# Writing out the two rounds of each kind of layer, one behind the other, on every engine

## The reference

```python
for l in range(DEPTH):            # first kind
    h = rms_norm(x, attn_norm_g[l]); proj = h @ w_in[l]            # 1024 x 3584
    ret = retention_bidir(...)      # 8 heads, with decays
    da = diff_attention(...)        # 4 heads, two softmaxes each
    x = x + concatenate([ret, da]) @ w_out[l]
    h = rms_norm(x, ffn_norm_g[l])
    x = x + (silu(h @ w_gate[l]) * (h @ w_up[l])) @ w_down[l]      # 2816 wide
for l in range(DEPTH):            # second kind
    # four branches (three kinds of attention and a convolution of 31 taps),
    # each gated and projected, then w_o
    x = x + sum(gates * proj) @ w_o[l]
    x = x + square(relu(rms_norm(x) @ w_up[l])) @ w_down[l]        # 4096 wide
return rms_norm(x, g_final)
```

## Time and profile before

| | before |
|---|---|
| time, median of 3 runs | 1469.72 us (1469.54 to 1470.15) |
| the profiled execution's own time | 1470.93 us |
| its span | 1469.1 us |
| TensorE (PE) busy | 1443.7 us, 98% of the span |
| weight loads (PEld) busy | 1202.3 us, 82% |
| VectorE busy | 942.9 us, 64% |
| ScalarE busy | 782.5 us, 53% |
| GpSimd busy | 95.9 us, 7% |
| granted TensorE clock | 0.998 of full speed |

### The profile page before, as it was taken

One profiled execution on the slowest core, in us unless ns is written; L12 is line 12 of the kernel. 1 busy time (PEld: TensorE's weight loads), 2 busy tenths in 40 slices (PEclk: granted clock), 3 DMA queues, 4 the chain that ended last, 5 costly groups with the idle time before them and its releaser, 6 DMA issues.

```text
span 1469.1 us, 21875 instructions
## 1 busy us (share of the span) xinstructions
PE 1443.7 (98%) x7107; PEld 1202.3 (82%) x7107; DVE 942.9 (64%) x1120; ACT 782.5 (53%) x1013; POOL 95.9 (7%) x112
## 2 busy tenths in 40 slices
PE   8999999999999999999999999999999999999997
PEld 6788888888788888887888888888878888888885
DVE  5765655446756555446788878755366888787644
ACT  6665544446855444446675555544366765565442
POOL 0211000002111000000210000000002200000000
PEclk9999999999999999999999999999999999999999
DMA  8533755555435655545454666555454556665641
GB/s 319 172 127 115 229 184 188 181 185 171 148 112 175 197 186 178 186 144 190 144 166 158 204 205 201 189 188 181 160 183 135 167 160 192 204 212 186 201 143 43
DMA packets 173641, 257.48 MB, mean 175 GB/s; under 512 B 8456, under 2 KB 92002, under 8 KB 173410
## 3 DMA queue, kind: packets, MB, share of 16 engines
q1 hardware_dynamic: 170432, 249.74, 52.2%
q10 hardware_dynamic: 2962, 5.95, 1.3%
q0 software_dynamic: 144, 0.52, 0.1%
HBM read 255.13 MB, written 1.05 MB: 174 GB/s over the span
## 4 chain that ended last, share of the span: by engine, by line
PE 72%; issue 23%; DVE 2%; ACT 1%; POOL 1%; DMA 0%; ACTq 0%; POOLq 0%; DVEq 0%
PE bank L501 19%; PE bank L503 18%; PE bank L502 18%; PE bank L977 4%; PE bank L535 4%; PE bank L976 2%; PE bank L666 1%; PE bank L518 1%; PE bank L520 1%; PE bank L519 1%; PE bank L623 1%; PE bank L649 1%; ACT w_hi L1039 1%; PE bank L640 0%; PE bank L816 0%
## 5 line engine op out<-in xcount | busy, mean ns | idle before, releaser
L1536 DVE TENSOR_TENSOR w_lo<-w_raw,w_hi 128x2048 fp32r<-128x2048 f32 (+2 forms) x250 | 545.6, 2187 | 223.0 <-ACT w_hi L1039 219.7
L1039 ACT CAST w_hi<-w_raw 128x2048 fp32r<-128x2048 f32 (+2 forms) x250 | 454.2, 1825 | 227.8 <-PE bank L503 203.9
L501 PE MATMUL bank<-w_hi,hT 128*128 128x512 f32 (+1 forms) x1056 | 418.6, 396 | 0.9 <-issue 0.7
L503 PE MATMUL bank<-w_hi,hT 128*128 128x512 f32 (+1 forms) x1056 | 411.2, 389 | 0.0
L502 PE MATMUL bank<-w_lo,hT 128*128 128x512 f32 (+1 forms) x1056 | 410.8, 389 | 0.0
L501 PEld LDWEIGHTS bank<-w_hi,hT 128*128 128x128 f32 x1056 | 198.8, 188 | 41.6 <-issue 3.0
L503 PEld LDWEIGHTS bank<-w_hi,hT 128*128 128x128 f32 x1056 | 198.6, 188 | 41.4
L502 PEld LDWEIGHTS bank<-w_lo,hT 128*128 128x128 f32 x1056 | 199.0, 188 | 37.9
L977 PE MATMUL bank<-hT,w_hi 128*128 128x512 f32 x512 | 178.1, 396 | 0.4 <-DVE sum L2091 0.4
L976 PE MATMUL bank<-hT,w_lo 128*128 128x256 f32 x448 | 125.1, 279 | 0.0
L2151 POOL TENSOR_TENSOR stat<-stat,cst 128x2 f32<-128x2 f32 (+3 forms) x23 | 45.8, 1992 | 1151.3 <-DVE stat L1585 1012.8
(11 more groups left out here) (269 smaller groups left out, 1643.3 us busy)
## 6 DMA issues: line engine op xcount, KB each, us to landing
w_raw<-in_w_gate SPq DMA_DIRECT2D x108, 512.0 KB, 4.0
w_raw<-in_w_up SPq DMA_DIRECT2D x108, 512.0 KB, 4.7
w_raw<-in_w_down SPq DMA_DIRECT2D x104, 512.0 KB, 4.4
w_raw<-in_w_in SPq DMA_DIRECT2D x88, 512.0 KB, 4.5
w_raw<-in_w_out SPq DMA_DIRECT2D x16, 512.0 KB, 4.2
w_raw<-in_w_branch SPq DMA_DIRECT2D x32, 256.0 KB, 3.0
w_raw<-in_w_o SPq DMA_DIRECT2D x16, 512.0 KB, 4.6
bgate<-in_b_gate ACTq DMA_DIRECT2D x16, 256.0 KB, 3.6
```

The source lines that it names most:

```text
L501: pe.matmul(o, hi[:, kt, rows_of(r)], w_hi[:, s, j, 0:cols], start=begin, stop=False)
L503: mm = pe.matmul(o, lo[:, kt, rows_of(r)], w_hi[:, s, j, 0:cols], start=False, stop=end)
L1039: act.copy(w_hi[:, s, 0:kts, :], w_raw[:, s, 0:kts, :]).then_inc(hi_ready, 1)
L1536: dve.tensor_tensor(w_lo[:, s, 0:kts, :], w_raw[:, s, 0:kts, :], w_hi[:, s, 0:kts, :].bitcast(F32), ALU.subtract).then_inc(lo_ready, 1)
```

## The change

`Place` gets a second generator, `layers`, which runs the body of a layer twice in Python and makes no loop of the hardware. All ten outer loops (two on each of SP, PE, ACT, DVE and POOL) use it in place of `rounds`; the arguments stay, and serve only for an assertion. The inner loops still use `rounds`. So `l` is a plain number, the counts on which the engines wait are constants outside the inner loops, slices such as `gcols[:, bass.ds(l * 16 + kt, 1)]` have a constant place, and there is no jump at a layer's end.

```diff
--- before.py
+++ after.py
@@ -174,6 +174,14 @@
         self.base = base
         self.k = {x: k.get(x, 0) + n * per.get(x, 0) for x in {*k, *per}}
+
+    def layers(self, per):
+
+        for l in range(DEPTH):
+            k = dict(self.k)
+            yield l
+            grown = {x: self.k[x] - k.get(x, 0) for x in self.k if self.k[x] != k.get(x, 0)}
+            assert grown == {x: y for x, y in per.items() if y}, (self.e, grown, per)
@@ -396,7 +404,7 @@
-            for l in q.rounds(DEPTH, dict(slab=len(KTS1))):
+            for l in q.layers(dict(slab=len(KTS1))):
@@ -610,7 +618,7 @@
-            for l in q.rounds(DEPTH, dict(slab=len(KTS1), blk=BLOCKS1, turn=TURNS1, scores=16, dve=9)):
+            for l in q.layers(dict(slab=len(KTS1), blk=BLOCKS1, turn=TURNS1, scores=16, dve=9)):
...
```

More of the change, by code:

```diff
@@ L423, in _ @@
                         slab(*rows(w["w_down"], k0, min(4, 22 - k0), b * NB, NB))
-            for l in q.rounds(DEPTH, dict(slab=len(KTS2))):
+            for l in q.layers(dict(slab=len(KTS2))):
                 w = {n: t[n + "_2"][bass.ds(l, 1)].rearrange("o k n -> (o k) n")
@@ L791, in _ @@
             q.next("probs", DEPTH * DH)
-            for l in q.rounds(DEPTH, dict(slab=len(KTS2), blk=BLOCKS2, turn=TURNS2, scores=12, pool=2, dve=6, hid=UPS,
+            for l in q.layers(dict(slab=len(KTS2), blk=BLOCKS2, turn=TURNS2, scores=12, pool=2, dve=6, hid=UPS,
                                           layer_in=64, probs=12, conv=1, out=3)):
@@ L1123, in _ @@
             loop4 = dict(slab=4, used=4, blk=2, **{f"in{s}": 16 for s in range(RING)})
-            for l in q.rounds(DEPTH, per1):
+            for l in q.layers(per1):
                 ahead = iter(KTS1[AHEAD:] + KTS1[:AHEAD])
@@ L1308, in _ @@
                         **{f"in{s}": 16 * len(KTS2) // RING for s in range(RING)})
-            for l in q.rounds(DEPTH, per2):
+            for l in q.layers(per2):
                 ahead = iter(KTS2[AHEAD:] + KTS2[:AHEAD])
@@ L1662, in _ @@
             loop4 = dict(slab=4, used=4, blk=2)
-            for l in q.rounds(DEPTH, dict(slab=len(KTS1), used=len(KTS1), blk=BLOCKS1, turn=TURNS1,
+            for l in q.layers(dict(slab=len(KTS1), used=len(KTS1), blk=BLOCKS1, turn=TURNS1,
                                           turn_hi=4 + 4 + 11 + 4, squares=9, rstd=7, act_done=11, scores=16,
@@ L1839, in _ @@
                 add_x(1)
-            for l in q.rounds(DEPTH, dict(slab=len(KTS2), used=len(KTS2), blk=BLOCKS2, turn=TURNS2,
+            for l in q.layers(dict(slab=len(KTS2), used=len(KTS2), blk=BLOCKS2, turn=TURNS2,
                                           turn_hi=2 + 4 + 4 + 4 + 4, squares=5, rstd=4, act_done=10, hid=UPS, scores=12,
@@ L2161, in _ @@
             pool.wait_ge(ident_in, 16)
-            for l in q.rounds(DEPTH, dict(mean=7, outputs=2, decay=RH, blk=BLOCKS1, step=STEPS_POOL1)):
+            for l in q.layers(dict(mean=7, outputs=2, decay=RH, blk=BLOCKS1, step=STEPS_POOL1)):
                 def diagonals(heads):
@@ L2192, in _ @@
                 q.next("blk", BLOCKS1)
-            for l in q.rounds(DEPTH, dict(mean=4, blk=BLOCKS2, step=STEPS_POOL2)):
+            for l in q.layers(dict(mean=4, blk=BLOCKS2, step=STEPS_POOL2)):
                 root_x()
```

## The result

| | before | after |
|---|---|---|
| median | 1469.76 us (1469.16 to 1470.2, 6 runs) | 1476.35 us (1473.9 to 1479.31, 6 runs) |
| ratio after / before | | 1.0043 (95%: 1.0032 to 1.0054) |
| the profiled execution's own time | 1470.93 us | 1479.31 us |
| its span | 1469.1 us | 1477.5 us |
| granted clock in it | 0.998 | 0.995 |

The changed kernel is 0.43% slower: 6.6 us more, where 1.5 us less had been forecast. The result lies outside the range.

What follows compares the result with a forecast made beforehand. PE was taken to bound the kernel; 1.06 us from its jumps plus 0.5 us from register instructions and waits made 1.56 us, so 1468.2 us from the median 1469.72, range 1466.0 to 1470.3, counted as no change.

Steps and rivals of the forecast that it cites:

- What bounds the kernel, and the gap at 1051 us: TensorE busy 1443.7 of 1469.1 us, clock granted in full; PE's weight loads lose 1.04 us to a jump at layer's end.
- PE's two jumps back: At the ends of PE's two first layers: removing the jumps gains 1.04 + 0.02 = 1.06 us, bounds 0 and 1.06.
- The jumps of the other engines: Layer ends on SP, ACT and DVE: removing these jumps is worth 0, being covered; uncovered, up to 4.6 us.
- Register instructions and constant waits: Hand-overs to PE: some 1250 instructions removed shorten six slow places by 0.08 us each, 0.5 us gain, bounds 0 and 3.2.
- Added code: PE's program grows from 5810 to 10984 instructions: costs 0, or 1.04 us if a new block came late once.
- Inner loops: Loops inside the layers keep the same bodies at other places of the program: taken as 0.
- slower: Rival, 8%: PE's short inner-loop jumps become long, each uncovering 1.04 us; all twelve give 1480.6 us.
- The waits are worth more: Rival, 10%: hand-overs shorten by more than 0.08 us as ACT and DVE lose register instructions; at the bound 1465.4 us.
- Nothing comes back: Rival, 20%: the gap at 1051 closes, but PE waits at the next hand-over instead; 1469.3 to 1469.8 us.
- The signs named at its end: Changed profile: no PE jump over 1 us, busy time within 1 us, span 1 to 2 us shorter, named waits within 0.1.

Runs made afterwards that it cites:

- experiment 3: Outer loops written out on PE alone, all other engines as in the kernel before: 1469.73 us, ratio 0.9993.
- Experiment 4: The changed kernel with ACT's outer loops kept as hardware loops, all other engines written out: 1469.82 us, ratio 0.9996.
- 1: The changed kernel with one ACT semaphore increment between the two waits of every gate: 1470.6 us, ratio 0.9999.
- 6: The changed kernel with the gate's two waits written in the other order, no instruction added: 1469.11 us, ratio 0.9992.
- 5: Outer loops written out on ACT alone, all other engines as in the kernel before: 1478.15 us, ratio 1.0061.
- 7: The changed kernel with an ACT semaphore increment between the two waits in only the first of a layer's eight gates: 1474.44 us, ratio 1.0030.
- 11: The changed kernel with an ACT semaphore increment between the two waits in gates 2 to 8, not the first: 1471.88 us, ratio 1.0014.
- experiment 2: The kernel before, loops kept, with an ACT semaphore increment behind both waits of the gate, so the table load follows both: 1475.79 us, ratio 1.0041.

## Why the prediction was wrong, point by point

- **What bounds the kernel, and the gap at 1051 us**: right. PE sets the time, and the gap was the jump. That the clock is "granted in full in every slice" reads too much into the page, whose digit 9 means 90% or more: the changed kernel's page has a 9 in every slice too, with two low stretches in it.
- **PE's two jumps back, 1.06 us of gain**: right at its place, 1.04 us shown in the changed kernel, and gone in experiment 3 too. Of the whole kernel's time the median of 3 shows a gain of 0.0007 of it, 1.0 us, with an interval that includes nothing.
- **The jumps of the other engines, 0**: nothing in these runs speaks against it. Experiment 4 takes them away on SP, DVE and POOL, together with PE's, and reads as 3 does.
- **"Register instructions and constant waits", +0.5 us, bounded by 0 and 3.2 us of gain**: this is the step that failed. It priced register instructions by the time that they take, and asked only how quickly a released wait gets through. It did not ask which instruction a wait moves to when the one that carried it is gone. At ACT's gates the late wait moved ahead of a table load of 1.28 us, twelve times. The loss of 6.6 us isn't in the bounds since no bound had a loss in it. The two bits of evidence could be had: ACT's rows of the program's order at the gate, and the overlap at 723.11 us in the trace of before; ACT's rows were read at the start of the first kind of layer alone, where the fold of five `ISA` and one `REGISTER_ALU` was taken as a gain. The prediction's small term itself came out as reckoned where the gates don't disturb it. At the gated sum the hop from DVE's signal to PE is 0.04 us where the earlier trace rows had 0.12, and PE's idle time there is 0.54 us in experiments 1, 4 and 6 where it was 0.61; at the hidden sum it is 0.44 where it was 0.51. What the term left out beside this: at the branch the same kernels stand 1.85 to 1.87 us where it was 1.71.
- **Added code, 0**: right. Experiment 3 has PE's 10984 instructions and loses nothing, and product follows product at the steady pace.
- **Inner loops, 0**: right, 76 to 240 ns.
- **The rivals**: "slower" had the right sign and the wrong mechanism (long jumps in inner loops; none is there). "The waits are worth more" expected the hand-overs to shrink as ACT loses register instructions; the opposite came. "Nothing comes back" is how the change would read with the gate's waits in order: experiments 1 and 6 come out within 0.1% of before.
- **The signs named at its end**: the jumps came out as said. PE's busy time and the span did not (3.1 and 8.4 us more). The waits on L1561 and `abias` were to keep within 0.1 us and did about (in all 2.9 us after 2.6, and 1.2 after 1.1); the list missed the waits for `qB` and `soft`, where the loss was.
- **Not foreseen at all**: that stalls can be followed by a stretch at the low clock. In the profiled execution it makes 1.6 us in each of the two layers.

What is shown: the loss is ACT's (4, 5), it is the gates' (1, 7, 11), it is which of two waits the table load carries (2, 6). The waits alone make 2.6 us a layer, 5.2 in two, less the jump's 1.0 us: 4.2 of the 6.6 us. Only argued: that the rest of the median is the clock. The slowest two of the changed kernel's six runs have a granted clock of 0.995 (1477.53 and 1479.31 us), the fastest two 0.998 (1473.9 and 1475.29); in experiment 2 the same loss came with no low clock in its profile, but with longer stalls. Why one execution falls to the low clock and another with the same stalls doesn't (the changed kernel and 11, 1 and 6) stays open.

## What to carry to other kernels

An instruction that only works out a number can still be the place where a wait is served. When a change removes such instructions, read for each engine which instruction each wait stands on, before and after, and look first at table loads and other preparing work that must not stand behind the late wait. Where two waits meet ahead of one, write the late one so that it falls to the instruction that needs it: with the order of the waits (here the late one first), or with a cheap instruction between them. An engine that is half idle isn't safe from this: at two hand-overs of each layer 0.92 and 1.14 us of the 1.28 us of delay went straight to the busy one.

## What the runs showed of the hardware

- **A stall can cost more than itself, but doesn't each time.** Behind stalls of 1.53 and 1.85 us within 5 us, TensorE ran for 3.3 us at the lower of its two clock levels, with a granted clock of 0.91 over 720 to 740 us; its price was 1.6 us. Experiments 1, 3, 4 and 7 show it once each in their profiles, behind the branch's stall (1.76 to 1.87 us) with only 0.55 to 0.60 us ahead of it. The profiles of 2, 5, 6, 11 and before don't show it there, though 2 has stalls of 1.70 and 1.71 us and 11 those of the changed kernel. So the length of these stalls doesn't decide it.
- **Of two waits written ahead of an activation with a table load, the last written is served before the table load, the first with the activation**, wherever no instruction stands between them (the changed kernel, 5 and 6: the load begins behind `term` at 724.92 and 724.99 us, and beside it at 721.89). The order of the waits in the code is all that differs between the changed kernel and 6.
- **Long jumps hide well.** Of jumps that held PE's sequencer for 3.3 and 4.4 us, the trace without them shows 1.04 us back; nearly twice as much code on PE cost nothing that a run could tell (experiment 3, 0.9993).
